# Two two-layer blocks on one core: the same instructions in another merged order of ten lanes

## The reference

```python
h = rms_norm(x, norm_gain[layer])
proj = h @ w_in[layer]
...
y_a = dsa_attention(q_a, k_a, v_a, q_i, k_i, w_i) * jax.nn.silu(z_a)
...
y_b = (rms_norm(o_b, gdn_norm_gain[layer])
       * jax.nn.silu(z_b.reshape(B, S, GDN_HEADS, GDN_DV))).reshape(B, S, GDN_WIDTH)
mixed = gates[:, :, 0, :] * y_a + gates[:, :, 1, :] * y_b
x = x + mixed @ w_out[layer]
```

```python
h = x @ w_in
...
for n in range(N_BRANCHES):
    yb = branches[n].reshape(b, s, BRANCH_WIDTH) * jax.nn.silu(gate_z[:, :, n])
    merged = merged + merge_g[:, :, n] * (yb @ w_branch[n])
out = merged @ w_out
return _layer_norm(DEEPNORM_ALPHA * x + out, ln_g, ln_b)
```

## Time and profile before

| | us |
|---|---|
| median of 3 runs | 1072.7 |
| lowest, highest | 1070.96, 1073.44 |
| the profiled execution: its time | 1073.65 |
| the profiled execution: its span, first to last instruction | 1071.6 |
| PE busy in the span | 1035.5 |
| POOL, DVE, ACT busy | 665.2, 605.4, 577.6 |

### The profile page before, as it was taken

One profiled execution on the slowest core, in us unless ns is written; L12 is line 12 of the kernel. 1 busy time (PEld: TensorE's weight loads), 2 busy tenths in 40 slices (PEclk: granted clock), 3 DMA queues, 4 the chain that ended last, 5 costly groups with the idle time before them and its releaser, 6 DMA issues.

```text
span 1071.6 us, 18457 instructions
## 1 busy us (share of the span) xinstructions
PE 1035.5 (97%) x7136; PEld 890.8 (83%) x7136; DVE 605.4 (56%) x1225; ACT 577.6 (54%) x972; POOL 665.2 (62%) x286
## 2 busy tenths in 40 slices
PE   8999999999989999999999998999999989999986
PEld 8987998878877987899888887788888778888865
DVE  4576365875584356465674654325557560545574
ACT  4754257734654575237655653446486535457651
POOL 4876456663557877437665546786446948735583
PEclk9999999999999999999999999999999999999998
DMA  8654434643325655334544434575334647514460
GB/s 281 215 160 121 137 99 138 177 136 121 119 99 151 189 171 162 110 99 133 156 145 126 132 99 132 148 226 142 89 96 132 197 126 210 152 54 124 119 196 39
DMA packets 80581, 151.57 MB, mean 141 GB/s; under 512 B 6448, under 2 KB 12400, under 8 KB 80496
## 3 DMA queue, kind: packets, MB, share of 16 engines
q1 hardware_dynamic: 80496, 150.41, 47.2%
HBM read 149.34 MB, written 1.05 MB: 140 GB/s over the span
## 4 chain that ended last, share of the span: by engine, by line
PE 88%; DVE 7%; ACT 2%; issue 1%; POOL 1%; DMA 0%; SPq 0%; DVEq 0%; ACTq 0%; POOLq 0%
PE bulk L926 52%; PE bulk L911 13%; PE chain L947 5%; PE chain L955 4%; PE chain L1033 4%; PE chain L1310 2%; PE chain L1291 1%; PE chain L1179 1%; PE chain L1163 1%; DVE arena L1835 1%; PE chain L1024 1%; PE bulk L919 1%; ACT w_hi L1350 1%; ACT arena L1350 1%; POOL w_lo L855 1%
## 5 line engine op out<-in xcount | busy, mean ns | idle before, releaser
L855 POOL TENSOR_TENSOR w_lo<-raw,w_hi 128x1024 fp32r<-128x1024 f32 (+4 forms) x277 | 651.4, 2372 | 383.1 <-ACT w_hi L1350 382.5
L1350 ACT ACTIVATE w_hi<-raw 128x1024 fp32r<-128x1024 f32 (+4 forms) x277 | 278.2, 1020 | 208.2 <-PE bulk L926 166.0
L926 PE MATMUL bulk<-w_hi,hT_hi 128*128 128x512 f32 (+1 forms) x756 | 307.7, 407 | 1.4 <-issue 1.1
L926 PE MATMUL bulk<-w_hi,hT_lo 128*128 128x512 f32 (+1 forms) x756 | 295.1, 390 | 0.0
L926 PE MATMUL bulk<-w_lo,hT_hi 128*128 128x512 f32 (+1 forms) x756 | 203.3, 389 | 1.3 <-POOL w_lo L855 1.2
L926 PEld LDWEIGHTS bulk<-w_hi,hT_hi 128*128 128x128 f32 x756 | 143.1, 189 | 34.2 <-issue 2.6
L926 PEld LDWEIGHTS bulk<-w_lo,hT_hi 128*128 128x128 f32 x756 | 141.5, 188 | 31.5 <-POOL w_lo L855 2.9
L926 PEld LDWEIGHTS bulk<-w_hi,hT_lo 128*128 128x128 f32 x756 | 143.0, 189 | 26.8 <-issue 1.0
L911 PE MATMUL bulk<-hT_hi,w_hi 128*128 128x256 f32 x384 | 96.2, 289 | 0.0
L911 PE MATMUL bulk<-hT_lo,w_hi 128*128 128x256 f32 x384 | 94.0, 283 | 0.0
L1350 ACT ACTIVATE arena<-chain 128x512 f32<-128x512 f32 (+5 forms) x68 | 46.3, 696 | 74.0 <-PE chain L947 33.2
(11 more groups left out here) (268 smaller groups left out, 1386.7 us busy)
## 6 DMA issues: line engine op xcount, KB each, us to landing
raw<-in_w_in_dram SPq DMA_DIRECT2D x194, 512.0 KB, 3.6
raw<-in_w_out_dram SPq DMA_DIRECT2D x32, 512.0 KB, 3.6
raw<-in_w_branch_dram SPq DMA_DIRECT2D x16, 512.0 KB, 3.9
raw<-in_w_mem_kv_dram SPq DMA_DIRECT2D x8, 512.0 KB, 3.5
raw<-in_w_merge_up_dram SPq DMA_DIRECT2D x16, 256.0 KB, 2.8
raw<-in_w_in_dram SPq DMA_DIRECT2D x8, 420.0 KB, 3.4
gain<-in_ln_rows_dram SPq DMA_DIRECT2D x4, 512.0 KB, 6.0
gain<-in_gains_dram SPq DMA_DIRECT2D x3, 512.0 KB, 6.5
```

The source lines that it names most:

```text
L855: pool.tensor_tensor(lo_of(p, u)[:, 0:n], raw_of(p, u)[:, 0:n], hi_of(p, u)[:, 0:n].bitcast(F32), ALU.subtract).then_inc(p.done("split"), 1)
L926: m = pe.matmul(dst, a, part[:, k, :], start=(first and not low and k == 0 and i == 0), stop=(last and low and k == nk - 1))
L1350: return act.activation(dst, src, func, **more)
```

## The change

All twelve lines of the string `ORDER` are replaced; it has the same 1178 letters of each kind, and nothing else in the file differs. Every engine issues the same instructions as before. Two of its lines, the first and the last:

```diff
@@ -320,18 +320,18 @@
 ORDER = (
-    "aaaaasavmmsssamaammssassaaaaccmmsccssaamcsaccsmmaacssmmaaccmsmmamcsssaaaadssmmaabaammssbsmsmammaaabd"
...
-    "byyvvsssdssmmdsyvmvdvmsmmmvvsyvvsdvvmmmmsssmvsvyvvsssmsvmveememmmvvvmvmemmmmee"
+    "aaaaasammvaamssmmsssaaaaaasccscscmmmssaacaccassmmammcssaaccmmcsmasssmamaaaamaaammmsdssasabssbbmmmmca"
...
+    "bsssyydvvssdsmmdymmvvssvvvvvsmmdmmvsvymssvmvsmmmsyvvvvssseeemmvmmmmmvvvmemeemm"
 )
```

More of the change, by code:

```diff
@@ L333 @@
-    "msmbabbsssmmamsssddaaabbsdammbbbbdbsmbmaaabssvmbbssmasbdmmabbmsbddssassmaybbmmmassbmdmyyadbmsvsbymyd"
-    "byyvvsssdssmmdsyvmvdvmsmmmvvsyvvsdvvmmmmsssmvsvyvvsssmsvmveememmmvvvmvmemmmmee"
+    "aaaaasammvaamssmmsssaaaaaasccscscmmmssaacaccassmmammcssaaccmmcsmasssmamaaaamaaammmsdssasabssbbmmmmca"
+    "aaadaasdabssmsssaaaaamaammbmaamaadmaaasmssassbammcaamcsssscmabbmaccccssbmaccmmmccsssaammbsbsmbbbambb"
+    "aasaamdassssacmmsaassdmmmmamaxmbaaassaaawdmssssadabmbbmbsswbxmmmssaaambmbbsaaabbmddsbbmsaamasssamxaa"
@@ new lines @@
+    "amwwamamwasxdmabssmaxssmdaxwbxmsaxxxbmbbmxaxssvvmmssmssmmmssaaammmaasadssssssmmmvmmaammaaccsscssmamm"
+    "accccssaaacsmmsammmacccsamssaaaammmsssssadamasdammmssaabbbmmmaaacaasssaamasaasdaaaaamabbmadamabbsmms"
+    "saassmabbamaacmacmcasssmcccacsssmmsmccscmacmmsabbmssambbbaaasssamaamdaammmssbabmmcmssdaaadaaaasssbbm"
+    "mbmxswassdsmmmssbbbmaaaaambmbssbmxdsssbbbmswbmaaammbsawxmaawwddsmmaaaxsmabsassxmaamasbadxbbmmmxswxxx"
+    "xxsssssssvvsmmmaamammmmamaasssasasdassmmmmsssmmmmddmmmsmmssbssdmmbsabmaasmmssbassmbdamassddmsambbaaa"
@@ L335 @@
+    "amsbbbdbsmbbssmaaabsmambbssmmddvabmsmsbbsbdmybssbmaamybmbdamyydavsssbysdsmsdssbyydmmvvyssdvvsvmsvmmm"
+    "dmmvvymmmvsvvvvsssssssmmmyvvvveemmmmmsevmmsmmvvvsesmeaaemmmmaammssmmmmmmsssmmsadbsmsdssmdamsabsaasmm"
+    "mambbdmbsssmdaasbbsmaaaamssbbbbddmmbsbmaaabsssmbbsmabmmdabbvssmbddasssmaybmsbsasmmbmmyaddybvssmbyydm"
+    "bsssyydvvssdsmmdymmvvssvvvvvsmmdmmvsvymssvmvsmmmsyvvvvssseeemmvmmmmmvvvmemeemm"
 )
```

## The result

The changed kernel is slower: its median is 1076.36 us (1075.83 to 1077.46, 5 runs) against 1072.7 (1070.96 to 1073.44, 5 runs), a ratio of 1.0039, 95% interval 1.0028 to 1.005. Forecast were 1065.8 and a range up to 1071.5.

The account below looks back on a forecast made before the run. TensorE, busy 97% of the span, was taken as the bound. The terms summed to -6.9 us, giving 1065.8 against the median 1072.7, with a range of 1061 to 1071.5.

Parts of the forecast that it names:

- Stretches: TensorE's runs of steps using part of the array: 18 fewer, at 0.33 us each, -5.9 us.
- Turnarounds: Waits for VectorE and ScalarE between inversion steps now in a row, in all four head groups: +1.8 us.
- h4.0: Second network, layer 1: this unit's wait for its late low part goes, -1.1 us.
- start of layer 1: Second network: ScalarE's square root of row 1 now precedes the copies turning row 0, +1.2 us.
- Rival B: Turnarounds eat the joins' gain, layer 0's end unchanged: 1070.8 us, at the edge of no change; chance 0.18.
- End of layer 0: First network: pv10 and o0.0 ahead of memT0 shorten the waits at pv10 and mT1, -1.8 us.
- End of the last layer: Unit o0.2 covers gT1's wait, 2.7 us, but o0.0 starts about 1.7 later: net -1.1 us.
- Rival C: GpSimd locks VectorE out at inversion turnarounds; eight holds add 9.6 us: 1075.4 us, slower; chance 0.08.
- Rival D: Two GpSimd holds or the clock's falls go as well, 2.2 + 1.7 us: 1062 us; chance 0.12.
- Clock: Fall to 1.2 GHz behind the last layer's wait stays: 0 in the sum, 1.7 us in the range.

Follow-up runs that it names:

- r14_one: Kernel before, with one extra step of eight 64x64 matmuls ahead of the first unit of 36 tiles of the first network: 1097.97 us.
- r15_two: Kernel before, with two extra steps of eight 64x64 matmuls in a row at each of the same 36 places as r14_one: 1111.92 us.
- r12_best: Changed kernel, first network's layer 0 end and part of layer 1 in the old order, last layer and second network's layer 1 start mended: 1067.1 us.
- r5_o11: Changed kernel, with the delta rule steps u11 and o11 at the end of layer 0 one weight unit earlier: 1076.91 us, ratio 1.0046.
- r6_end: Changed kernel, with the drains and merges of br21 and br31 in the last layer put behind gT0 on VectorE: 1073.96 us, ratio 1.0018.
- r9_tail2: Changed kernel, with the end of layer 0 from unit g10.6 to mT1 in the order of before: 1073.94 us, ratio 1.0014.
- r7_start: Changed kernel, with the second network's first two layer 1 xT steps put ahead of layer 0's last drain and moments: 1075.09 us, ratio 1.0027.
- r11_end2: Changed kernel, with the last layer up to unit br01.0 in the order of before and o0.2 kept ahead of gT1: 1072.73 us, ratio 1.0007.
- r13_two2: First network in the order of before, second in the changed order with its layer 1 start and last layer mended: 1065.77 us, ratio 0.9934.
- r16_kvb: As r13_two2, with unit kvb.0 of the second network's layer 0 ahead of sbi0 on TensorE: 1067.62 us, ratio 0.9942.
- r4_short: Changed kernel in its own order, with GpSimd's subtraction cut from 1024 to 64 columns for eight units: 1068.77 us, ratio 0.9967.

## Why the prediction was wrong

- **Stretches, -5.9: right.** -5.3 in the ledger, 0.31 to 0.37 for a join by the traces of r14_one and r15_two. TensorE's busy time did not show it in the changed kernel, against what I had said, since time at the lower clock counts as busy; in r12_best it is 1030.0, 5.5 below before, of which some 3 are two falls of the clock fewer.
- **Turnarounds, +1.8: right**, as are h4.0 and the start of layer 1. Rival B did not happen.
- **End of layer 0, -1.8: the step that failed first.** I asked which wait each move took away, and not what else the two moved steps had covered: o0.0 needs mT0's low part whatever stands between (r5_o11), and memT0 was part of that cover. Measured +1.1, and 2.7 of clock with it in the profiled execution.
- **End of the last layer, -1.1: wrongly sized**, +0.7. I took off a drain "that is no longer in the way". It is in the way: gT0's subtraction now stands behind two pairs of gating and adding, and the gating that had released o0.0 before still comes first (1037.35). The wait went from 0.8 to 4.2, by the add and the subtraction in full, and not to 2.5.
- **What was missing, and the largest: invY101 and invY111, +3.4.** I counted turnarounds inside the joined stretches, and not the halves of `chain` that a stretch takes from the steps ahead of it. The joined steps follow the scores by one unit, where before invY101 stood ahead of sc00.
- **Rival C, given 0.08, is the mechanism, at other places.** I priced a hold at 1.2 us on the answers inside the inversion. These read PSUM and none was held, as I had said against it. The holds fell on SBUF-only operations (the mask behind top-k, the gate product, o11's last) in front of the answers, up to 2.2 us each, and several in a row. The case reached "slower" with two such places and not eight, since the holds there added up to waits of 3.6 and 3.0 us and each wait brought the clock down, and since the last layer's end cost instead of saving.
- **Rival D** came true for the two holds at sbo1 (-2.6) and for one fall of the clock, that at 762 behind the first of them, which did not offset this.
- **Clock: 0 taken, 1.7 in the range; measured +3.2** in the profiled execution: 2.7 and 2.2 at the two new waits, less 1.7 for the fall that went. I left the falls that new waits can bring out of the sum. They are no sure cost of a wait either: at pv10 every order with the wait had a fall, of 6.8 us or of 3.4, and at invY111 some executions had none.

Open: why one of two waits of the same length is followed by a fall and another is not. invY111's wait of 2.7 us had a fall of 6.8 us in the changed kernel, r5_o11 and r6_end, of 3.4 in r9_tail2 and none in r7_start and r11_end2. mT1's wait of 2.9 us in layer 1 had one in the kernel before and in r13_two2 and none in r16_kvb, r4_short and r12_best. Each kernel has one profiled execution, so how much of this goes with the order and how much with the execution is not shown; part of the scatter between runs comes from there, and sums of edits are uncertain by some 2 us.
